# Two expert steps with fixed places ahead of the routing table, in a two-layer hybrid diffusion kernel

## The reference

```python
scores = sigmoid(t @ router_w); sel = scores + router_b
best = argmax(sum of the two best sel in each group of 4 experts)
idx = top_k(sel inside the best group, 2)
gates = one_hot(idx) * scores / (sum of the two scores)
a = einsum('td,edf->tef', t, w_gate); b = einsum('td,edf->tef', t, w_up)
act = silu(a) * b * gates
x = x + gate2 * einsum('tef,efd->td', act, w_down)
```

## Time and profile before

| | us |
|---|---|
| median of 3 runs | 1068.78 |
| the runs | 1061.59, 1068.78, 1068.89 |
| profiled execution: time | 1064.19 |
| profiled execution: span | 1062.3 |
| PE busy in the span | 1016.3 |
| DVE busy | 622.1 |
| ACT busy | 399.7 |

### The profile page before, as it was taken

One profiled execution on the slowest core, in us unless ns is written; L12 is line 12 of the kernel. 1 busy time (PEld: TensorE's weight loads), 2 busy tenths in 40 slices (PEclk: granted clock), 3 DMA queues, 4 the chain that ended last, 5 costly groups with the idle time before them and its releaser, 6 DMA issues.

```text
span 1062.3 us, 20679 instructions
## 1 busy us (share of the span) xinstructions
PE 1016.3 (96%) x7322; PEld 551.9 (52%) x7323; DVE 622.1 (59%) x1318; ACT 399.7 (38%) x811; POOL 207.6 (20%) x309
## 2 busy tenths in 40 slices
PE   4999999999999889999999999999999988999997
PEld 1666555554544454555456655555654435445442
DVE  0344455656535886666574545466734687677667
ACT  1332214444311126666443222354531113666660
POOL 0133458000000010010142435800000001100013
PEclk9999999999999999999999999999999999999999
DMA  9960006677800579999980000477250168999938
GB/s 378 356 176 1 1 0 235 270 292 269 316 20 40 197 277 409 418 418 418 379 305 7 1 0 1 168 310 272 96 218 20 40 218 320 421 416 418 412 153 294
DMA packets 70739, 237.90 MB, mean 224 GB/s; under 512 B 11176, under 2 KB 26688, under 8 KB 56336
## 3 DMA queue, kind: packets, MB, share of 16 engines
q1 hardware_dynamic: 58720, 195.36, 47.7%
q0 software_dynamic: 6480, 23.60, 6.1%
q10 hardware_dynamic: 5472, 18.12, 4.2%
HBM read 211.53 MB, written 25.53 MB: 223 GB/s over the span
## 4 chain that ended last, share of the span: by engine, by line
PE 81%; DMA 7%; DVE 5%; issue 3%; POOL 2%; SPq 1%; ACT 1%; DVEq 0%; POOLq 0%; ACTq 0%
PE pair L1088 13%; PE bank L1170 12%; PE pair L803 8%; PE pair L1197 7%; PE pair L818 7%; PE pair L938 5%; PE bank L713 4%; PE pair L835 4%; PE bank L852 4%; PE bank L974 3%; PE bank L953 3%; DMA big<-ada_w 3%; DMA big<-w_down 2%; PE pair L1136 2%; PE bank L787 2%
## 5 line engine op out<-in xcount | busy, mean ns | idle before, releaser
L1170 PE MATMUL bank<-big,actT 128*32 (+2 forms) x1168 | 178.6, 379 | 3.9 <-DVE big L2300 2.2
L1504 ACT ACTIVATE actT<-big 128x1024 f32 x138 | 144.3, 1055 | 71.3 <-PE bank L1170 26.8
L1170 PE MATMUL bank<-actT 128*32 128x256 f32 x1840 | 164.7, 379 | 0.0
L1088 PE MATMUL pair<-big,actT 128*128 128x512 f32 x320 | 142.7, 598 | 0.0
L1170 PEld LDWEIGHTS bank<-big,actT 128*32 128x32 f32 (+1 forms) x1168 | 98.9, 114 | 81.7 <-issue 23.2
L1088 PEld LDWEIGHTS pair<-big,actT 128*128 128x128 f32 x320 | 59.0, 190 | 67.8 <-issue 67.6
L803 PE MATMUL pair<-big,actT 128*128 128x384 f32 (+1 forms) x320 | 93.7, 447 | 0.2 <-ACT actT L1261 0.2
L2031 DVE TENSOR_REDUCE mx<-pair 128x1 f32<-128x640 f32 x64 | 52.6, 823 | 66.8 <-PE pair L939 66.6
L1197 PE MATMUL pair<-big 128*32 (+2 forms) x384 | 91.0, 595 | 0.7 <-ACT big L1519 0.7
L1170 PEld LDWEIGHTS bank<-actT 128*32 128x32 f32 x1840 | 86.5, 110 | 0.0
L2300 DVE COPY big<-big 128x1024 f32 x92 | 63.4, 689 | 35.8 <-PE bank L1170 28.0
(11 more groups left out here) (304 smaller groups left out, 1632.1 us busy)
## 6 DMA issues: line engine op xcount, KB each, us to landing
big<-ada_w SPq DMA_DIRECT2D x48, 1024.0 KB, 6.4
big<-w_gate SPq DMA_DIRECT2D x32, 1024.0 KB, 9.5
big<-w_up SPq DMA_DIRECT2D x32, 1024.0 KB, 9.6
big<-w_down SPq DMA_DIRECT2D x32, 1024.0 KB, 9.9
y_rows<-big ACTq DMA_DIRECT2D x24, 512.0 KB, 7.7
big<-w_out SPq DMA_DIRECT2D x4, 2048.0 KB, 10.1
big<-mod_rows SPq DMA_DIRECT2D x16, 512.0 KB, 7.2
h_rows<-big ACTq DMA_DIRECT2D x10, 512.0 KB, 2.7
```

The costliest lines, as they stand in the source:

```text
L1088: m = mm(dst, actT[:, k, t * P:(t + 1) * P], vw.wo[n][:, k, :], start=(k == order[0]), stop=(k == order[-1]))
L1170: m = mm(dst[lo:lo + m_, 0:DE], xgT[:, k, lo:lo + m_], weights(c, k % 4 * DE, DE), start=(k == 0), stop=(k == DC - 1), tile_position=(0, l ...
L1504: f(parts[1][i % 3], slot[:, i * PIECE:(i + 1) * PIECE], ACT.Copy).then_inc(w_a, 1)
```

## The change

**Fixed steps.** The steps 0 and 1 serve experts 0 to 3, one for each quarter, 32 rows each. Step 0 takes the first 32 places of each from tiles 0 to 2 alone: PE counts these places in the middle of the last product of the projection (`first_places`, `first_rows`), and the gather goes to a place of its own (`xg_first`) from h2's first 384 rows. Step 1 takes the next 32 of each from all tiles. The table starts at chunk 8 with what is left, with least numbers of chunks set anew (expert 4 three, 5, 7, ... two). In both steps PE reads all weights in the ring itself, and ScalarE makes both halves of the copy for steps 1 and 2; VectorE copies half of the turned rows of step 0 only. PE's order puts counting and lists between the pieces of the products; the dummies there go.

**Loads.** Expert 1 is asked for after the pools' products, gate and up of 2 at product 9, and the rest piecewise: gate 3 after `op_x`, up 3 after `h_gain`, down 2 after `r_pt`, down 3 after `h_ready`, gate and up 4 after `op_mm`, down 4 after `r_slot`. Places in the ring are 1, 2, 3, 0, 4.

On VectorE `activation(0)` stands some operations behind the second index, the output scaling of step 0 behind the lists, `activation(1)` behind `r_fin`, and the place formula of `eslot` has four operations more.

**Rows of h2** are written in order; turning them reads every eighth word (`by_k`). **The row gates** of tokens move into step 2 (`token_gates`), the gate difference ahead of the table. POOL waits for expert 13's step at the end of layer 0, SP for 14's ahead of w_in's pool part.

```diff
+PLACES = (1, 2, 3, 0, 4)
+FIXED = 2
+NFIX = 4
+NT_FIRST = 3
...
-    least[:, 0] = -1
-    least[1::2, 1] = -1
-    least[0, 0:FIRST_CHUNKS] = -1
+    least[1:NFIX, 1] = 0
+    least[NFIX:, 0] = -1
+    least[NFIX + 1::2, 1] = -1
+    least[NFIX, 0:3] = -1
...
-        def by_row(a, lo=0, hi=P):
-
-            return a.rearrange("q (k p) -> q p k", k=DC)[:, lo:hi, :]
-
-        def plain(a):
-
-            return a.rearrange("q (p k) -> q p k", k=DC)
+        def by_k(rows):
+
+            return rows.rearrange("q (p k) -> q k p", k=DC)
...
                 load_expert(0)
+                sp.wait_ge(s_pv, L(s_pv) + 1 + NGRP)
+                spread(vw.S, 3 * l + 1, D, ld_sg)
                 sp.wait_ge(pool_d, L(pool_d) + NG)
                 sp.wait_ge(pool_mm, L(pool_mm) + NG)
+                load_expert(1)
                 sp.wait_ge(op_mm, L(op_mm) + 2 * NT - 1)
-                load_expert(1)
+                load_gate(2)
+                load_up(2, None)
+                sp.wait_ge(op_x, L(op_x) + 2 * NT)
+                load_gate(3)
                 sp.wait_ge(op_g, L(op_g) + 2 * NT)
                 spread(gate, 3 * l + 2, D, ld_gate)
+                sp.wait_ge(h_gain, L(h_gain) + 1)
+                load_up(3, None)
                 sp.wait_ge(r_pt, L(r_pt) + NT)
-                sp.wait_ge(moe_in[l], 16)
-                load_expert(2)
-                sp.wait_ge(op_x, L(op_x) + 2 * NT)
-                sp.wait_ge(r_gate, L(r_gate) + 1)
+                load_down(2, None)
+                sp.wait_ge(h_ready, L(h_ready) + 2 * NT)
+                load_down(3, None)
+                sp.wait_ge(op_mm, L(op_mm) + 2 * NT)
+                load_gate(4)
+                load_up(4, None)
                 sp.wait_ge(r_slot, L(r_slot) + 1)
-                load_expert(3)
-                load_expert(4)
+                load_down(4, None)
...
+                def first_places():
+
+                    pe.wait_ge(r_mask, L(r_mask) + 1)
+                    mm(pos_f[:, 0:NT_FIRST, :], k16("upto"), mask16[:, 0:NT_FIRST, :], start=True, stop=False, skip_group_check=True)
+                    for i in range(NT_FIRST):
+                        after = NT_FIRST - i
+                        m = mm(pos_f[:, i + 1:i + 1 + after, :], k16("ones16"),
+                               mask16[:, i, :].unsqueeze(1).broadcast_to([P, after, NE]), start=False,
+                               stop=(i == NT_FIRST - 1), skip_group_check=True)
+                    m.then_inc(r_tot, 1)
+
+                def first_rows():
+
+                    pe.wait_ge(r_one, L(r_one) + 1)
+                    pe.wait_ge(op_g, L(op_g) + 2 * NT - 2)
+                    for t in range(NT_FIRST):
+                        m = mm(rows_f, list_f[t], k16("token")[:, t:t + 1], start=(t == 0), stop=(t == NT_FIRST - 1))
+                    m.then_inc(r_pe1, 1)
...
+                        if j == 2 * NT - 1 and k == 2:
+                            first_places()
+                        if j == 2 * NT - 1 and k == 5:
+                            first_rows()
...
-                stay_awake(pair[1][:, 0:HALF], 4)
-                pe.wait_ge(r_mask, L(r_mask) + 1)
-                pe.wait_ge(op_g, L(op_g) + 2 * NT)
...
-                stay_awake(a7, 4)
-                stay_awake(a7, 3)
...
+                def fixed_rest(n):
+
+                    turn_act(n, 0)
+                    turn_act(n, 1)
+                    pe.wait_ge(b_yd, n + 1)
+                    down(n, 0, fixed_weights(4))
+                    pe.wait_ge(g_in, n * 16 + 32)
+                    turn_rows(range(DC)).then_inc(b_t, 1)
+                    down(n, 1, fixed_weights(5))
 
                 pe.sem_inc(used, USED_0)
+                pe.wait_ge(op_g, L(op_g) + 2 * NT)
...
-                turn_rows(range(DC)).then_inc(b_t, 1)
+                turn_rows(range(DC), xg_first).then_inc(b_t, 1)
+                pe.wait_ge(b_ta, 1)
+                pe.wait_ge(b_td, 1)
+                gate_up(0, fixed_weights(0))
+                gate_up(1, fixed_weights(1))
+                all_places()
+                gate_up(2, fixed_weights(2))
+                second_rows()
+                gate_up(3, fixed_weights(3))
+                fixed_rest(0)
+                pe.wait_ge(b_ta, 2)
+                pe.wait_ge(b_td, 2)
+                gate_up(0, fixed_weights(0))
+                gate_up(1, fixed_weights(1))
                 list_rows()
-                land_0, place_0 = landed(l, 0), slice(slot_of(0), slot_of(0) + 1)
-                products(0, land_0, place_0, True)
+                gate_up(2, fixed_weights(2))
+                gate_up(3, fixed_weights(3))
+                fixed_rest(1)
                 pe.wait_ge(r_slot, L(r_slot) + 1)
                 pe.wait_ge(r_fin, L(r_fin) + 1)
                 n_more = pe.value_load(n_more_s[0:1, 0:1], min_val=NSTEP_MIN - 1, max_val=NSTEP - 1)
-                rest(0, land_0, place_0, True, False)
...
+                def rows_copies(n):
+
+                    rows_copy(n)
+                    f(xgT[:, 4:8, :], pair[0][:, HALF:2 * HALF].rearrange("p (k n) -> p k n", n=P), ACT.Copy).then_inc(b_td, 1)
...
+                fixed_step(0)
+                store_y(0)
+                fixed_step(1)
+                act.wait_ge(r_fin, L(r_fin) + 1)
+                act.wait_ge(r_slot, L(r_slot) + 1)
+                part = part_place(FIXED)
+                for i in range(3):
+                    part_copy_w(FIXED, part, i)
+                store_y(1)
...
+                for t in range(NT - 1):
+                    row_rs2(t)
+                pool.wait_ge(h_st[0], L(h_st[0]) + 16 * 2)
+                pool.wait_ge(h_st[1], L(h_st[1]) + 16)
+                pool.wait_ge(r_idx, L(r_idx) + 1)
+                nc.gpsimd.indirect_dma_start(
+                    xg_first, None, h2_rows[0:NT_FIRST * P, :], bass.IndirectOffsetOnAxis(ap=idx[:, 0:1], axis=0))\
+                    .then_inc(g_in, 16)
+                row_rs2(NT - 1)
                 pool.wait_ge(h_st[0], L(h_st[0]) + 16 * 3)
                 pool.wait_ge(h_st[1], L(h_st[1]) + 16 * 2)
-                pool.wait_ge(r_idx, L(r_idx) + 1)
-                gather(0)
                 pool.wait_ge(r_idx, L(r_idx) + 2)
                 gather(1)
+                pool.wait_ge(r_idx, L(r_idx) + 3)
+                gather(2)
...
+                    h2 = xn[t % 2]
+                    link(v.scalar_tensor_tensor(h2, x[:, t, :], rs[:, NT + t:NT + t + 1], vw.G[:, c2, :], ALU.mult, ALU.mult))
+                    if t == NT - 2:
+                        first_slots()
+                    v.tensor_tensor(h2, h2, vw.S[:, c2, :], ALU.add).then_inc(h_ready, 1)
+
+                def first_slots():
+
+                    ve.wait_ge(r_tot, L(r_tot) + 1)
+                    v.tensor_scalar(fix_u, pos_f[:, NT_FIRST, 0:NFIX], float(CH), None, ALU.min)
+                    link(v.tensor_tensor(slot_f, pos_f[:, 0:NT_FIRST, 0:NFIX], mask16[:, 0:NT_FIRST, 0:NFIX], ALU.mult))
+                    in_row = k16("row")[:, 0:CH].unsqueeze(1).unsqueeze(1).broadcast_to([P, NT_FIRST, NFIX, CH])
+                    v.tensor_tensor(onep_f, in_row, slot_f.unsqueeze(3).broadcast_to([P, NT_FIRST, NFIX, CH]), ALU.is_equal)\
+                        .then_inc(r_one, 1)
...
+                ve.wait_ge(op_mm, L(op_mm) + 2 * NT)
+                rows_copy(1)
                 select(3, 3, NT).then_inc(r_mask, 1)
                 b_t, b_ta, b_td, b_sil, b_act, b_at, b_atc, b_sel, b_yd, used, b_st, b_end, *w_s = by_layer[l]
-                ve.wait_ge(r_tot, L(r_tot) + 1)
-                pos = o6[:, 0:NT * NE].rearrange("p (t e) -> p t e", e=NE)
-                link(tt(slot_0, pos[:, :, 0], mask16[:, :, 0], ALU.mult))
-                tt(onep[:, 0:NT, :], k16("row").unsqueeze(1).broadcast_to([P, NT, P]), bc(slot_0, P), ALU.is_equal)\
-                    .then_inc(r_one, 1)
-                tot = o6[:, NT * NE:(NT + 1) * NE]
-                link(tt(least, bc(tot, NTOK // CH), k16("least").rearrange("p (e k) -> p e k", k=NTOK // CH), ALU.is_gt))
+                ve.wait_ge(ld_gate, 64 * l + 64)
+                link(tt(gate[:, 0, :], gate[:, 0, :], gate[:, 1, :], ALU.subtract))
+                ve.wait_ge(r_tot, L(r_tot) + 2)
+                link(v.tensor_copy(places, pos_all))
+                pos, tot = places[:, 0:NT, :], places[:, NT, :]
+                pos_x = places[:, 0:NT, 0:NFIX]
+                each_tile = lambda q: q.unsqueeze(1).broadcast_to([P, NT, NFIX])
+                link(tt(beyond, pos_x, each_tile(fix_u), ALU.subtract))
+                link(tt(slot_g, beyond, mask16[:, :, 0:NFIX], ALU.mult))
+                tt(onep_g, k16("row")[:, 0:CH].unsqueeze(1).unsqueeze(1).broadcast_to([P, NT, NFIX, CH]),
+                   slot_g.unsqueeze(3).broadcast_to([P, NT, NFIX, CH]), ALU.is_equal).then_inc(r_one, 1)
+                ts(fix_v, fix_u, -1.0, float(P), ALU.mult, ALU.add)
```

(16 more changed lines are left out.)

387 lines of the change are left out of this document (220 added, 167 removed).

## The result

The changed kernel takes 1082.61 us in the median of four runs (1079.39 to 1087.84), the kernel before 1067.93 on the same chip: a ratio of 1.0155 (95%: 1.0097 to 1.0213). It is slower, by 15 us, where I forecast 8 less. The profiled execution took 1087.84 us with a span of 1086.0, 23.7 more than before. PE begins the projection of layer 0 at 284.68 where it was 283.43, ahead of every edit that could delay it, so some 22.4 are to be found. So stretches are compared, not times from the start. And the profiled execution is the slowest of the four: its stretches add up to more than the 15 us between the medians.)

The account below looks back on a forecast made before the run. PE, busy 96% of the span, was taken as the bound, with weights close behind. Terms 3.8 + 7.2 - 0.6 - 0.3 - 2.0 = 8.1 us took 1064.2 to 1056.1 as profiled, 1060.7 for the median; range 1046 to 1080.

Parts of the forecast that it names:

- worth nothing within the projection (PE bounds it): Output projection: contiguous norm2 and gain_half save some 0.7 us each on VectorE, but gain nothing there.
- The end of the projection: Layer 0: last projection matmul begins its drain at 359.55, leaving a 20.9 us hole before step 0's products at 380.47.
- First product at 368.2: Start of step 0, layer 0: first product about 368.2, 12.3 us earlier than before; range 367.5 to 372.5.
- Step 1's products at 387.5: Layer 0: expert 3's down weights at 381.5, second gather landing at 384.6, then turning and half a down.
- Rival 2: No gain, 1068: third gather too takes 8.3 us (+3.5 a layer), or gate rows land late; chance 0.22.
- Step 1 to step 2 in 15.0 us: Layer 0: list, third gather and table put step 2's products at 402.5, against 408.24; 5.7 us earlier in each layer.
- The weights afterwards: Layer 0 after step 2: late place release gives back 1.8 us; step 10 at 499.8 instead of 503.63, gain 3.8.
- The 7.2 of layer 1: Layer 1's gain: 5.7 us from earlier step 2 plus 1.5 from the drift going.
- the present drift: Layer 1: nine steps take 108.94 us where 9 x 11.94 = 107.5; later first uses of experts would remove it.
- POOL's extra place load: 0.3: End of layer 0: an additional place load on POOL costs 0.3 us.
- Rival 1: turn_rows' transposes: strided weight loads of 0.252 us add 28 us less some 2 of slack, 1087; chance 0.18.
- rival 3: Full cover: second gather in 4.2 to 6 us, no clock dips, 1053; ceiling step 2 at 392.4, about 1040; chance 0.18.

Follow-up runs that it names:

- c4_free: Changed kernel: S row's own semaphore, expert 4's gate/up after second gather, gate row behind expert 3's w_down, later gate subtraction, experts 0-3 loads not waiting for one another; 0.9929.
- c7_load: c4_free with place matmuls a quarter earlier; at layer 0's end GpSimd's register load precedes all waits, expert 13's gate half awaited, stored rows last; ratio 0.9919.
- a_half: Changed kernel loading only the first half of gate and up for experts 5 to 15, so outputs are not the layer's; ratio 1.0096 to the kernel before.
- a_byrow: Changed kernel with h2 rows written in permuted order and turned from contiguous columns, as before; ratio 1.017 to the kernel before.
- c1_quiet: Changed kernel with the S row on its own semaphore and expert 4's gate and up asked for only after the second gather landed; ratio 1.0025 to the kernel before.
- c3_awake: c1_quiet with gate row behind expert 2's w_down, gate subtraction just ahead of the first step's gate row, and 16 dummy matmuls in step 0; ratio 1.025.

## Why the prediction was wrong

**A move that I didn't price: the S row.** This is the largest step that failed, a term put at nothing without a reason. Of SP's queue the prediction prices the weights and the gate row; for the S row, which the change moves behind expert 0's 3 MB and the last attention product, it has no term. The two transfers leave at 283.03 and land at 292.5, beside loads of experts 0 and 1. VectorE's wait `ld_sg >= 80 * (l + 1)` ahead of the gains still counts them; behind that wait stand the two gains (2.36) and off2 (`off` in the rows), for whose small matmul PE waits between its first and second product (from 291.8, so a landing by about 289.2 would have done). It costs 6.7 us in layer 0 (3.9 of waiting beyond the start's shift, 2.8 at the low clock) and 4.0 in layer 1 (2.3 and 1.7), 10.7 together; two single edits, one each way, show 10 and 9 us. With it alone priced, the forecast would have been 1071. It was also out of sight in "worth nothing within the projection (PE bounds it)": I looked for bounds inside the projection and not at its gate.

**The end of the projection.** The last product does not begin its drain at 359.55; two matmuls more run, to 360.6. So the hole that the change attacks was 19.8 us, not 20.9. Behind the S row's part 0.3 us are left in each layer for the seven small matmuls of the first places, where I took 0.65.

**First product at 368.2.** 7.8 us behind the projection's end in the trace, 6.9 in the forecast. The wait is for w_gate, as said; from its issue to the first product it took 6.3 us, where I took 5.4, with the shortest landing of 4.7 in it.

**Step 1's products at 387.5.** Late by 8.9 us against the projection's end, nearly all in three terms of 3.4, 2.6 and 2.6. The second index was to leave 14.6 us behind it and left 18.0 behind (386.88): VectorE waited 2.05 us for the gate row, and then 1.55 for PE, held up by expert 3's w_up, for which I had no term and which took 12.70 us to land beside that row. The second gather took 10.58 us where I took 8.0 from the pairing of before; with expert 4's loads held back it takes 5.9. And the low clock added 0.9 to the turning and 1.7 to a down product: 2.6 us, where I took 1.0 of a range to 2.7. Rival 2 had the late gate row, but with the third gather, which nobody waited for.

**Step 1 to step 2 in 15.0 us.** 14.8 measured. List, third gather and table are hidden, as argued.

**The weights afterwards.** The mechanism, that fixed experts hold their places until step 2, was in the prediction, and so was the wait at step 10 in layer 0. The term was too small: from step 2 to step 10 it gives 97.3 us, and the changed kernels of the table take 99.1 to 102.0; the 1.3 in it "to start an idle queue" stands in no row, and no run shows it by itself. Another 1.6 to 2.9 at the low clock behind the wait had no term. I gave back 1.8 us; where steps 0 and 1 come as early as I said (c4_free to c7_load) all of the gain is given back by the end of layer 0's steps.

**The 7.2 of layer 1.** From its projection's end layer 1 gains 1.6. The late steps 0 and 1 take most: step 2's products come 46.4 us behind the projection's end, where 41.2 was forecast. The 1.5 for "the present drift" did not come either: the nine steps from step 2's down to step 11's take 108.7 us, before 108.94, and 109.4 in a_half, where an expert has 2 MB to load instead of 3. So the drift stays when weights come sooner, and what makes it is not shown.

**"POOL's extra place load: 0.3."** It is 3.7 us. Of my two readings one, the waited event, fell by a test: with the wait shortened the gather stays where it was. With the register load ahead of the waits and the waits in another order the delay is gone, 0.9 us behind the store in place of 6.1. What in the 4.8 us between the last wait and the gather takes the time stays open.

**Rival 1** was refuted. I had bounded a strided load at 252 ns, from VectorE's writes; it takes 194 (before 141, in a_byrow 151), and eight transposes take at most 0.07 us more. The Trainium skill (SBUF — State Buffer, "SBUF cachelines") would have each word of such a row pay for a line of its own; the load is indeed 43 to 53 ns longer, and next to nothing of that comes out on the path. The slower side came true all the same, by a mechanism that was not on my list.

**The steps** (12 and 13, 3200 matmuls), the steady pace and win_p were right. (The ceiling in rival 3 adds up to 392.1, not 392.4, which changes nothing.)

What stays open, beside the two points above: one profiled execution of each kernel differs from another by a few us, so shares below 1 us in the tables are not shown by a second trace.

## What to carry to other kernels

When the order of a DMA queue changes, price each transfer that is moved by its waiter: who counts its semaphore, and what stands behind that wait. A transfer issued early costs others that are needed sooner; hold back what nobody needs until the small one that everybody waits for has landed (10.6 to 5.9 us for the gather here). And when an early start makes a ring of buffers full sooner, nothing is won until the ring's first release moves too: find the load from which the tail's rate runs, and count from that.

## What the runs showed of the hardware

- An indirect gather of 128 rows took 10.58 us beside 3 MB of weights issued within 1 us of it, and 5.9 in c1_quiet, with 2 of the 3 MB held back.
- A 1 MB weight load took 12.70 us when two others and the gate row were in flight, against 4.7 at best.
- Turning rows with every eighth word as weights loads in 194 ns instead of 141 to 151, and eight transposes take 1.14 to 1.16 us instead of 1.09.
- With a register load of 0.29 us behind the awaited store, a gather on GpSimd began 4.8 us after its last wait was passed (6.1 behind the store); with the load ahead of all waits, 0.8 (0.9 behind the store).
- In step 10 behind a wait for weights the granted clock was 0.54, and 128 matmuls took 9.65 us, where step 10 of the kernel before took 7.04.
- A float32 matmul of 512 columns shows as two matmuls of 0.43 us: 16 dummies took 13.93 us (c3_awake).
